# One expert-weight schedule, rearranged: the loads that lead into the first expert stage of a two-layer kernel on one core

## What is computed

```python
for layer in range(DEPTH):                       # DEPTH = 2
    if layer % 2 == 0:
        p = rms_norm(h, e_norm[i]) @ e_w_in[i]
        y_a = rwkv7_mix(p[..., :RWKV_IN], ...)
        y_b = rglru_mix(p[..., RWKV_IN:RWKV_IN + LRU_WIDTH], p[..., RWKV_IN + LRU_WIDTH:], ...)
        h = h + concatenate([y_a, y_b]) @ e_w_out[i]          # 1024 x 1024
    else:
        p = rms_norm(h, o_norm[i]) @ o_w_in[i]
        h = h + gla_mix(p, ...) @ o_w_out[i]
    h = h + hier_moe(rms_norm(h, m_norm[layer]), ...)

def hier_moe(h, ...):
    ...
    for e in range(N_EXPERTS):                   # 32
        hid = silu(hf @ w_gate[e]) * (hf @ w_up[e])           # 1024 -> 256
        y = y + (hid @ w_down[e]) * combine[:, e:e + 1]       # 256 -> 1024
```

## Time and profile before

| | us |
|---|---|
| median of three runs | 794.77 |
| lowest, highest | 793.01, 795.64 |
| the profiled execution, its own time | 795.4 |
| its span, first to last instruction | 792.7 |
| TensorE busy | 716.6 (90% of the span) |
| VectorE, ScalarE, GpSimd busy | 319.1, 205.6, 30.8 |

### The profile page before, as it was taken

The page is one execution under the profiler, slowest core; times in us unless marked ns, Lnnn a source line. Parts: engine busy times, 40 slices in busy tenths (PEclk is TensorE's granted clock), DMA queues, the critical chain, the costliest instruction groups (busy, mean ns, idle before and its releaser), DMA issues.

```text
span 792.7 us, 16704 instructions
## 1 busy us (share of the span) xinstructions
PE 716.6 (90%) x7436; PEld 456.6 (58%) x7436; DVE 319.1 (40%) x678; ACT 205.6 (26%) x414; POOL 30.8 (4%) x99
## 2 busy tenths in 40 slices
PE   8999999999989998999889999999998986877695
PEld 6778777658645564455537745884764543434342
DVE  6376876625353323333235054632445321221222
ACT  2574567215100000000032263540420000000003
POOL 7006000000000000000000000000000000000000
PEclk9999999999999998999999999999999998988998
DMA  8644113489999999999999613009999999999994
GB/s 261 197 104 141 55 55 110 166 342 378 396 421 420 421 420 421 420 420 421 411 330 370 225 62 102 1 8 408 421 386 422 420 421 420 421 420 421 421 403 159
DMA packets 69861, 242.14 MB, mean 305 GB/s; under 512 B 9814, under 2 KB 33484, under 8 KB 49052
## 3 DMA queue, kind: packets, MB, share of 16 engines
q1 hardware_dynamic: 69580, 240.52, 77.5%
q10 hardware_dynamic: 208, 0.54, 0.2%
HBM read 240.00 MB, written 1.05 MB: 304 GB/s over the span
## 4 chain that ended last, share of the span: by engine, by line
PE 54%; DMA 17%; DVE 5%; issue 3%; SPq 1%; PEld 1%; ACT 0%; PEldq 0%; ACTq 0%
DMA M<-in_m_w_down_dram 12%; PE ps L1806 11%; PE ps L1499 10%; PE ps L1345 7%; PE ps L1446 6%; DMA M<-in_m_w_gate_dram 4%; PE ps L1461 4%; PE ps L1571 4%; DVE H L2403 1%; PE ps L1360 1%; PE ps L1639 1%; PE ps L996 1%; SPq L425 1%; PE ps L1380 1%; PE ps L1645 1%
## 5 line engine op out<-in xcount | busy, mean ns | idle before, releaser
L1499 PE MATMUL ps<-M 128*32 128x256 f32 x2016 | 127.3, 403 | 19.2 <-DMA M<-in_m_w_gate_dram 14.1
L1499 PEld LDWEIGHTS ps<-M 128*32 128x32 f32 x2016 | 67.3, 116 | 77.0 <-issue 19.4
L1806 PE MATMUL ps<-M 128*128 128x256 f32 (+2 forms) x320 | 87.0, 428 | 1.0 <-DVE M L1937 1.0
L1045 PE MATMUL ps<-M 128*128 128x272 f32 x352 | 85.0, 396 | 2.8 <-DVE M L2078 1.8
L1446 PEld LDWEIGHTS ps<-M 128*128 128x128 f32 x608 | 71.5, 192 | 12.4 <-issue 12.0
L1446 PE MATMUL ps<-M 128*128 128x128 f32 x608 | 76.9, 278 | 0.0
L1045 PEld LDWEIGHTS ps<-M 128*128 128x128 f32 x352 | 65.7, 190 | 18.3 <-issue 2.9
L1806 PEld LDWEIGHTS ps<-M 128*128 128x128 f32 x320 | 59.7, 190 | 24.5 <-issue 16.7
L1461 PE MATMUL ps<-M 128*128 128x512 f32 (+1 forms) x120 | 60.6, 626 | 7.4 <-DVE H L2403 5.3
L1571 PE MATMUL ps<-M 128*32 128x512 f32 x448 | 55.1, 636 | 13.0 <-DMA M<-in_m_w_down_dram 13.0
L2400 DVE TENSOR_TENSOR H<-H,ps 128x512 f32<-128x512 f32 x60 | 41.2, 687 | 61.2 <-PE ps L1461 60.9
(11 more groups left out here) (454 smaller groups left out, 818.7 us busy)
## 6 DMA issues: line engine op xcount, KB each, us to landing
M<-in_m_w_gate_dram SPq DMA_DIRECT2D x32, 2048.0 KB, 18.0
M<-in_m_w_down_dram SPq DMA_DIRECT2D x26, 2048.0 KB, 21.8
M<-in_m_w_up_dram SPq DMA_DIRECT2D x25, 2048.0 KB, 20.9
M<-in_o_w_in_dram SPq DMA_DIRECT2D x12, 1024.0 KB, 8.9
M<-in_e_w_in_dram SPq DMA_DIRECT2D x11, 1024.0 KB, 6.0
M<-in_m_w_down_dram SPq DMA_DIRECT2D x9, 1024.0 KB, 18.4
M<-in_m_w_up_dram SPq DMA_DIRECT2D x8, 1024.0 KB, 18.6
M<-in_e_w_out_dram SPq DMA_DIRECT2D x4, 1024.0 KB, 5.3
```

The lines of the kernel that those rows point to most:

```text
L1045: ins = pe.matmul(ps[:, n % 4, 0:T], wringE[:, (n // 2) % 4, k, (n % 2) * P:(n % 2) * P + P], xnE[:, k], start=(k == 0), stop=(k == KD - 1))
L1499: ins = pe.matmul(ps[32 * e:32 * e + 32, 3 * x, 0:FF], xgT[q % 2][:, k, 32 * e:32 * e + 32], w, start=(k == 0), stop=(k == KD - 1))
L1806: ins = pe.matmul(ps[rows, unit % 4, 0:n], lhs(k), rhs(k), start=(k == 0), stop=(k == KD - 1))
```

## The change

It touches the loads that lead into the first expert stage, and what waits for them:

1. The output weights of the first layer are laid out and loaded as four quarters of 256 columns with all 1024 rows, not as two halves of the columns by two halves of the rows. A 512-wide product then reads its operand from two places 2048 words apart.
2. Experts 0 and 1 of unit 2 (down) are sent after the first `centred` (`oc_set` 1). Experts 2 and 3 stay at `sa_evac` 5 and `lru_in` 6.
3. Unit 0 (gate) waits for the last `centred` (`oc_set` 5). The wait for `mixE` 5 moves behind it, ahead of unit 1.
4. Of unit 3 the third expert (its place is the third column quarter) is sent after `res_done` 5, the fourth after `res_done` 6, behind the piece for `yst`. The third is counted by `ld_wout`, which TensorE waits for before unit 3.

```diff
--- before.py
+++ after.py
@@ -196,7 +196,7 @@
         rsB = W[:, 15 * SLAB + 9 * T:15 * SLAB + 10 * T]
         junk = W[:, 15 * SLAB + 10 * T:15 * SLAB + 10 * T + 3 * 512].bitcast(BF16).rearrange("p (t d) -> p t d", t=3)
         wringE = M[:, 0:8192].rearrange("p (s k c) -> p s k c", s=4, k=KD)
-        woutE = M[:, 0:8192].rearrange("p (h k d) -> p h k d", h=2, k=KD)
+        woutE = M[:, 0:8192].rearrange("p (g k d) -> p g k d", g=4, k=KD)
         wring = M[:, 0:10240].rearrange("p (s k c) -> p s k c", s=5, k=KD)
         wout = M[:, 37120:45312].rearrange("p (h k d) -> p h k d", h=2, k=KD)
 
@@ -332,9 +332,8 @@
             for g in range(8, 11):
                 load_w(g)
             for turn, j in enumerate((3, 0, 1, 2)):
-                h, ks = j // 2, slice(4 * (j % 2), 4 * (j % 2) + 4)
                 sp.wait_ge(s("proj_done"), 16 + 2 * turn)
-                sp.dma_start(woutE[:, h, ks], a["e_w_out"][0].rearrange("(k p) d -> p k d", p=P)[:, ks, 512 * h:512 * h + 512]) \
+                sp.dma_start(woutE[:, j], a["e_w_out"][0].rearrange("(k p) d -> p k d", p=P)[:, :, 256 * j:256 * j + 256]) \
                     .then_inc(s("ld_wout"), 16)
 
             def experts(y):
@@ -357,9 +356,12 @@
                     sp.dma_start(slots[j][:, 3, D:2 * D], src[:, 3, D:2 * D]).then_inc(s(rest), 16)
 
                 if y == 0:
+                    j = UNIT_SLOT[0][2]
+                    sp.wait_ge(s("oc_set"), 1)
+                    sp.dma_start(slots[j][:, 0:2, :], down[:, 0:2, :]).then_inc(s(f"ld_s{j}"), 16)
                     sp.wait_ge(s("sa_evac"), NC)
                     sp.wait_ge(s("lru_in"), 6)
-                    whole(2, down[:, 0:4])
+                    sp.dma_start(slots[j][:, 2:4, :], down[:, 2:4, :]).then_inc(s(f"ld_s{j}"), 16)
 
                 for u in range(NU):
                     q, kind = divmod(u, 3)
@@ -367,6 +369,7 @@
                     if y == 0 and u == 2:
                         continue
                     if y == 0 and u == 1:
+                        sp.wait_ge(s("mixE"), NC)
                         but_quarter(u, up[:, 0:4], "ld_pv_ys")
                         for e in range(2):
                             set_aside(e)
@@ -376,7 +379,7 @@
                             set_aside(e)
                     if u == 0:
                         if y == 0:
-                            sp.wait_ge(s("mixE"), NC)
+                            sp.wait_ge(s("oc_set"), NC)
                         else:
                             sp.wait_ge(s("mix_part"), 1)
                     elif u == 1 and y == 1:
@@ -384,9 +387,14 @@
                     elif u == 3:
                         sp.wait_ge(s("res_done"), (4, 9)[y])
                         sp.dma_start(slots[j][:, 0:2, :], gate[:, 4:6, :]).then_inc(s(f"ld_s{j}"), 16)
-                        sp.wait_ge(s("res_done"), 6 if y == 0 else 11)
                         if y == 0:
+                            sp.wait_ge(s("res_done"), 5)
+                            sp.dma_start(slots[j][:, 2, :], gate[:, 6, :]).then_inc(s("ld_wout"), 16)
+                            sp.wait_ge(s("res_done"), 6)
                             sp.dma_start(yst[0], up[:, 3, 0:D]).then_inc(s("ld_pv_ys"), 16)
+                            sp.dma_start(slots[j][:, 3, :], gate[:, 7, :]).then_inc(s(f"ld_s{j}"), 16)
+                            continue
+                        sp.wait_ge(s("res_done"), 11)
                     elif u == OV_NEXT:
                         if y == 0:
                             sp.wait_ge(s("ov_free"), passes)
@@ -1335,14 +1343,19 @@
                 for k in ks:
                     for g in range(4):
                         ins = pe.matmul(ps[32 * g:32 * g + META, BANK[0][4], 0:256], mixT[:, k, TOK[2]],
-                                        woutE[:, g // 2, k, 256 * (g % 2):256 * (g % 2) + 256], start=(k == 0), stop=(k == 7))
+                                        woutE[:, g, k, :], start=(k == 0), stop=(k == 7))
                 return ins
 
             def part(y, n, c0, w, bank, ks=range(8)):
 
                 for k in ks:
-                    w_out = (wout if y else woutE)[:, c0 // 512, k, c0 % 512:c0 % 512 + w]
-                    ins = pe.matmul(ps[:, BANK[y][bank], 0:w], mixT[:, k, TOK[n]], w_out, start=(k == 0), stop=(k == 7))
+                    res = ps[:, BANK[y][bank], 0:w]
+                    if y:
+                        w_out = wout[:, c0 // 512, k, c0 % 512:c0 % 512 + w]
+                    else:
+                        w_out = woutE[:, c0 // 256:(c0 + w) // 256, k, :]
+                        res = res.rearrange("p (g d) -> p g d", d=256)
+                    ins = pe.matmul(res, mixT[:, k, TOK[n]], w_out, start=(k == 0), stop=(k == 7))
                 if ks[-1] == 7:
                     ins.then_inc(s("res_done"), 1)
 
@@ -1479,6 +1492,8 @@
                     pe.wait_ge(s(f"ld_s{j}"), 32 * (FIRST_LAYER[j] * y + UNIT_TURN[y][u] + 1))
                     if y == 0 and u == 1:
                         pe.wait_ge(s("ld_pv_ys"), 272)
+                    elif y == 0 and u == 3:
+                        pe.wait_ge(s("ld_wout"), 80)
                     elif y == 0 and u == 5:
                         pe.wait_ge(s("ld_lruw_e5"), 96)
 
@@ -1877,7 +1892,7 @@
             from_state(4)
             spread_norm(1)
             summed(2)
-            pe.wait_ge(s("ld_wout"), 96)
+            pe.wait_ge(s("ld_wout"), 112)
             pe.wait_ge(s("mix_part"), 1)
             keep_busy(1, 0)
             spread_norm(2)
```

## The result

| | median us | lowest, highest | runs |
|---|---|---|---|
| before | 794.77 | 793.01, 796.12 | 7 |
| changed | 799.05 | 797.33, 801.13 | 7 |

The ratio is 1.0049, with a 95% interval of 1.003 to 1.0068: the change makes the kernel slower by half a per cent, 3.9 us by the ratio and 4.3 by the medians. The forecast of 793.8 and its range to 795.9 were wrong, and so was its likeliest case, no difference over 0.3%. The profiled execution of the changed kernel took 799.22 us, span 797.4 (before 792.7), mean granted clock 0.967 (before 0.973).

The account below looks back on a forecast made before the run. The prediction took the first expert stage's weight stream, at the DMA engines' rate, as the bound, to be won by an earlier start. Sum -1.0 us: 795.4 to 794.4 profiled, 793.8 after 0.6 us to the median; range 791.4 to 795.9.

Parts of the forecast that it names:

- likeliest case: Whole kernel: no difference over 0.3% (2.4 us) either way, chance 0.70.
- the early loads disturb the recurrence: Rival, chance 0.10: 2 MiB under the third and fourth chunks lengthen two chunks by 1.4 us; 796.6 us.
- The gate's issue and the 10 us: First expert stage: gate weights go at 151.9 instead of 162.94, putting their stream 10 us ahead.
- The holes and the restart: First expert stage's queue: holes at about 183, 187 to 191 and 200; a start from empty costs 1.8 us.
- the cut: Splitting the gate half of unit 3 in two, against the skill's rule to batch loads to 1 MiB or more.
- The gain of the rest: First expert stage's end: 2.8 us of queued work less 1.8 us for the restart, 1.0 us gained.
- the rival without a restart: First expert stage: the queue doesn't care about restarts, gain 2.2 to 2.6 us, 792.3 us; chance 0.24.
- 3.4 us of waits at the end: First expert stage's end: TensorE waits 1.5 us on a gate load and 1.9 us on the last down load.
- Nothing: Terms put at no cost: 1 KB output-weight rows hidden by cover, operand in two places, TensorE's extra wait on `ld_wout`.

Follow-up runs that it names:

- no early load: The changed kernel, but all of unit 2 (down) sent after `sa_evac` 5 and `lru_in` 6 as before: 793.57 us, ratio 0.999 to before.
- gate late: The changed kernel without the early down load and with the gate waiting for `mixE` 5 again: 794.81 us, ratio 0.9998 to before.
- quarter late: The changed kernel without the early down load, unit 3's third and fourth experts together after `res_done` 6, old `ld_wout` waits: 794.34 us, ratio 0.9987 to before.

## Why the prediction was wrong

**The step that failed** is the term that the sum put at nothing, the effect of the early down load on the recurrence. The forecast left `sa_evac` 5, `res_done` 6 and all behind them where they were; the runs showed them 5.8 us late, from 6.1 us lost in two chunks, because the load holds back a block of TensorE's instructions. It stood in the prediction only as the rival "the early loads disturb the recurrence". I gave it 0.10, with a price of 2 x 1.4 us, and wrote against it that the 512-wide matmuls of line 1345 take no longer under a full DMA load than those of line 1806. The row is right and answers another question: how long a matmul takes that has been issued. The load doesn't touch the operands, it holds up the instructions. And that row comes from a stretch with 26 matmuls and 24 weight loads in 4 us, while the recurrence has 153 and 156. With so few instructions there is one block in 24 us (160 to 184) against five (124 to 148). Had I compared the counts of the two stretches, and read TensorE's waits from 134 to 160 us for the label "issue", the 0.56 us at 135.94, right behind a weight load, would have pointed at the effect in the trace of before.

**Its price** was also too small: 2.8 us forecast, 6.1 measured. Of these 3.2 are the stop (0.56 in the old place stays as it was), 2.9 the clock at half. I had no term for the clock.

**The gate's issue and the 10 us** were right relative to the recurrence: 151.9 + 5.8 = 157.7, measured 157.69, and 163 to 165.5 us, which was weak before, is at full rate (it now lies 5.3 us behind the gate's issue):

```profile
163.00:165.50 2.50, 2.50 (x7) 1.10 (x6) 0.00 (x0) 0.00 (x0) 0.00 (x0) 1.00 1.01 426
191.00:194.00 3.00, 3.00 (x21) 2.72 (x20) 2.58 (x12) 3.00 (x2) 0.00 (x0) 1.00 0.56 197
```

**The holes and the restart** came as forecast, moved by 5.8 us: the queue runs empty ahead of `res_done` 6 (197 GB/s from 191 to 194, the second row above, and nothing at all from 195 to 196). The stretch of 3 us behind the issue at 205.04 moves 154 GB/s; against 426 that is a loss of 3 x (426 - 154)/426 = 1.9 us, where I had taken 1.8:

```profile
205.00:208.00 3.00, 2.93 (x40) 2.22 (x44) 1.69 (x9) 1.03 (x2) 0.00 (x0) 1.00 0.59 154
```

The Trainium skill's 0.6 us to the first byte ("DMA: Bandwidth & Descriptors", Latency and other measured facts) would have made the loss about a third of that, by estimate; the row decides against it as the price of a restart, as it is the time to the full rate that counts. The Trainium skill's rule of loads of 1 MiB or more (the same page, Bandwidth), which I let speak against the cut, has nothing against it: the two pieces are 1 MiB each.

**The gain of the rest**, forecast as 1.0 us, is 0.8 by the ratio of "no early load" (interval from 2.1 us faster to 0.6 slower) and 1.1 by the medians. The size fits; the account behind it fits less well. Counted from `res_done` 6, the matmuls that wait for the last down load start after 213.65 us (409.08 - 195.43) instead of 215.81 (405.41 - 189.60): the stream is 2.2 us ahead, not 1.0, nearer to the rival without a restart. The stage's end is 2.0 us ahead (229.96 against 231.93). Between the two, 1.5 us come from the clock, since these 16 matmuls took 3.43 us before, at half clock behind the 1.9 us of waiting, and 1.92 in the changed kernel; and the second wait of 1.65 us (above), a load later, takes it back. I had counted 3.4 us of waits at the end without asking what a wait does to the clock behind it, nor which load is late next. By the times alone 2 us is at the edge of the interval, and 1.0 in the middle of it. And in the prediction the third quarter's own release could win something only by the room that the early gate makes in the queue; the trace of "gate late" has the earlier end (229.9) without the early gate. Over all twelve kernels the shorter stage goes with the quarter's release (229.5 to 230.9 us against 231.9 to 232.7), and so does the missing extra fall of the clock. So the 10 us by which the gate's stream was ahead seem to have bought nothing, and the one load taken out of the batch the 2 us. That the clock's fall is a result of the late quarter, and not luck in three executions, isn't shown, and the times of "gate late" and "quarter late" differ by less than their intervals.

**Nothing** was right for the 1 KB rows, for the operand in two places and for the added waits: the 48 matmuls of 512 columns take 596 ns as before.

```profile
L1358 PE MATMUL ps<-M 128*128 128x512 f32 x48 | 21.1, 596 | 0.0
```

## What to carry to other kernels

Before a load is moved under work that the DMA engines had been quiet for, count the instructions of the engine beside it, not only the operands it reads. Where TensorE issues some 300 instructions in 4 us, its code is a stream with a deadline, and a weight load across a block can stop it; put such loads into the gaps between blocks, in pieces of 0.5 MiB, or leave them where instructions are few. In a trace, "issue" as the reason of a wait in the middle of a group of like instructions is the sign, and a granted clock of 0.50 behind it is the second half of the bill.

## What the hardware showed that I had not expected

- TensorE's instructions come in blocks of 16 KB over the DMA engines. From 124 to 148 us, 725 matmuls and 725 weight loads take five of them, about 290 for each; over the whole execution it is 252. In six stops TensorE goes on 2.4 to 2.8 us after its block moved (133.5 to 135.94 before, 140.0 to 142.80 changed, then 139.0 to 141.67, 139.5 to 141.93, 140.5 to 143.08, 146.5 to 149.23). There is hardly any margin: in "quarter late" the next block moved at 137.5, half a microsecond later than before and with no load beside it, and TensorE stopped for 0.16 us (until 139.94) after the same 11 matmuls. So not every small stop needs a load.
- The block that moves 1.8 us after the end of the first `centred` before (137.0 against 135.2) came 3.0 us behind the issue of a load of 0.5 MiB, 4.3 with 1 MiB, 4.7 and 5.0 with 2 MiB: 1.2, 2.5, and 2.9 to 3.3 us late. "DMA: Bandwidth & Descriptors" of the Trainium skill (Latency and other measured facts) gives 0.2 us of access latency to memory on average and 2 us at high load. That bears on it in direction; how a block of one queue is held by loads of another wasn't tested.
- The clock after a stop: 3.17 us, 2.63 and 2.08 were followed by stretches at or near half speed, and so was 1.38 (at 149.23, in other work); 1.53 wasn't. So the length of the stop alone doesn't decide it, and these runs don't tell what else does.
